# Recurrent stage of a two-block layer: next item's exponential, keys and mask work issued ahead of the current item's output work

## The reference, cut to what matters

```
def step(carry, inp):
    C, n, m = carry
    qc, kc, vc, ic, fc = inp
    b = jnp.cumsum(fc, axis=-1)
    d_log = jnp.where(causal, b[..., :, None] - b[..., None, :] + ic[..., None, :], -jnp.inf)
    m_inter = b + m[..., None]
    m_t = jnp.maximum(m_inter, jnp.max(d_log, axis=-1))
    w_intra = jnp.exp(d_log - m_t[..., None])
    w_inter = jnp.exp(m_inter - m_t)
    s = jnp.einsum('bhld,bhsd->bhls', qc, kc) * w_intra
    num = w_inter[..., None] * jnp.einsum('bhld,bhde->bhle', qc, C) + jnp.einsum('bhls,bhse->bhle', s, vc)
    den = w_inter * jnp.einsum('bhld,bhd->bhl', qc, n) + jnp.sum(s, axis=-1)
    h = num / jnp.maximum(jnp.abs(den), jnp.exp(-m_t))[..., None]
    ...
    C_new = decay[..., None, None] * C + jnp.einsum('bhs,bhsd,bhse->bhde', w_s, kc, vc)
...
hc_f, st_f = mlstm_chunkwise(qc, kc, vc, ifc, lfc, zero)        # context, forward
hl_f, _ = mlstm_chunkwise(ql, kl, vl, ifl, lfl, st_f)           # latent, from that state
...                                                             # and both reversed
out_lat = mlstm_output(hl_f + jnp.flip(hl_b, axis=2), p_lat, g_norm)
```

## Time and profile before

| | us |
|---|---|
| median of three runs | 3012.24 |
| the profiled execution, its own time | 3010.53 |
| its span (first to last instruction) | 3008.7 |
| TensorE busy over the span | 2878.0 (96%) |
| VectorE, ScalarE, GpSimd busy | 2046.6, 1243.9, 144.7 |
| recurrent stage, from its first instruction to the first one behind its barrier | 674.86 to 745.59 |
| of it TensorE's items b(0) to b(15) | 679.65 to 740.8 |
| mean granted TensorE clock over the span | 0.986 of full speed |

### The profile page before, as it was taken

The page is one execution under the profiler, slowest core; times in us unless marked ns, Lnnn a source line. Parts: engine busy times, 40 slices in busy tenths (PEclk is TensorE's granted clock), DMA queues, the critical chain, the costliest instruction groups (busy, mean ns, idle before and its releaser), DMA issues. The chain is left out here.

```text
span 3008.7 us, 38123 instructions
## 1 busy us (share of the span) xinstructions
PE 2878.0 (96%) x14307; PEld 2349.9 (78%) x14307; DVE 2046.6 (68%) x2904; ACT 1243.9 (41%) x2122; POOL 144.7 (5%) x225
## 2 busy tenths in 40 slices
PE   6999999998999999999999999998989999999997
PEld 2587667988778888788787888887878888887786
DVE  3368645837778889997895768774765756775455
ACT  3322535417454555454444332324444224445353
POOL 1100000001010000000001000000001001001000
PEclk9999999998999999999999999999999999999999
DMA  9877045841858778787785646662423544684333
GB/s 359 305 265 246 17 136 158 283 153 35 297 197 268 246 257 255 239 269 256 262 305 173 189 148 175 217 216 64 142 93 131 197 152 150 205 280 125 100 140 131
DMA packets 282967, 589.44 MB, mean 196 GB/s; under 512 B 31090, under 2 KB 64090, under 8 KB 279201
## 3 DMA queue, kind: packets, MB, share of 16 engines
q1 hardware_dynamic: 272384, 546.64, 55.4%
q0 software_dynamic: 10000, 39.72, 3.8%
q10 hardware_dynamic: 400, 0.66, 0.1%
HBM read 572.21 MB, written 14.72 MB: 195 GB/s over the span
## 5 line engine op out<-in xcount | busy, mean ns | idle before, releaser
L3137 DVE TENSOR_TENSOR w_lo<-raw,w_hi 128x1024 fp32r<-128x1024 f32 (+2 forms) x668 | 785.6, 1188 | 384.1 <-ACT w_hi L3108 375.0
L3108 ACT ACTIVATE w_hi<-raw 128x1024 fp32r<-128x1024 f32 (+2 forms) x668 | 677.8, 1031 | 879.9 <-PE bank L3200 630.9
L732 DVE SCALAR_TENSOR_TENSOR acc<-raw,sc_t,acc 128x1024 f32<-128x1024 f32 x480 | 601.8, 1281 | 44.1 <-DMA acc<-in_b_ada 25.1
L3198 PE MATMUL bank<-w_hi,l_hT_hi 128*128 128x512 f32 (+1 forms) x1056 | 390.5, 370 | 10.3 <-DVE w_lo L3137 9.3
L3200 PE MATMUL bank<-w_hi,l_hT_lo 128*128 128x512 f32 (+1 forms) x1056 | 386.9, 366 | 0.0
L3199 PE MATMUL bank<-w_lo,l_hT_hi 128*128 128x512 f32 (+1 forms) x1056 | 386.8, 366 | 0.0
L3198 PE MATMUL bank<-w_hi,f_hT_hi 128*128 128x512 f32 x704 | 278.2, 395 | 1.7 <-DVE mod L780 1.1
L3200 PE MATMUL bank<-w_hi,f_hT_lo 128*128 128x512 f32 x704 | 274.9, 390 | 0.0
L3199 PE MATMUL bank<-w_lo,f_hT_hi 128*128 128x512 f32 x704 | 274.8, 390 | 0.0
L3198 PEld LDWEIGHTS bank<-w_hi,l_hT_hi 128*128 128x128 f32 x1056 | 198.3, 188 | 51.4 <-DVE w_lo L3137 13.1
L3200 PEld LDWEIGHTS bank<-w_hi,l_hT_lo 128*128 128x128 f32 x1056 | 198.2, 188 | 31.5
(11 more groups left out here) (471 smaller groups left out, 4633.2 us busy)
## 6 DMA issues: line engine op xcount, KB each, us to landing
raw<-in_w_in SPq DMA_DIRECT2D x240, 512.0 KB, 4.8
raw<-in_w_mod SPq DMA_DIRECT2D x192, 512.0 KB, 5.5
raw<-in_w_ada SPq DMA_DIRECT2D x192, 512.0 KB, 4.7
raw<-in_w_up SPq DMA_DIRECT2D x176, 512.0 KB, 4.8
raw<-in_w_out SPq DMA_DIRECT2D x96, 512.0 KB, 4.8
raw<-in_w_down SPq DMA_DIRECT2D x88, 512.0 KB, 5.6
raw<-in_w_in SPq DMA_DIRECT2D x32, 288.0 KB, 3.4
raw<-in_w_ukv SPq DMA_DIRECT2D x32, 256.0 KB, 3.4
```

What stands on the lines that cost most here:

```text
L732: e.scalar_tensor_tensor(acc[a][:, :], raw[s % RAW_SLOTS][:, :], scalar, acc[a][:, :], ALU.mult, ALU.add).then_inc(fma_done, 1)
L3108: e.activation(slot(w_hi[u % SPLIT_SLOTS], g.width), slot(raw[s % RAW_SLOTS], g.width), ACT.Copy).then_inc(hi_ready, 1)
L3137: e.tensor_tensor(slot(w_lo[u % SPLIT_SLOTS], g.width), slot(raw[s % RAW_SLOTS], g.width), slot(w_hi[u % SPLIT_SLOTS], g.width).bitcast(F3 ...
L3198: e.matmul(o, xh[:, k, tok], hi[:, kk, :], start=first, stop=False)
```

## The change

Two loops are written in another order; nothing is added or removed, and no semaphore wait is changed. On ScalarE, `c(s-1)` (the scaling of the item before) moves from ahead of the exponential and the keys of item s+1 to behind them. On VectorE, `b(s+1)` (mask times products of the next item) moves from behind the sums of item s-1 to ahead of them.

```
             for s in range(-1, NCH + 2):
                 if s in (3, 5, 7, 9):
                     fill["act"](e, (s - 3) // 2)
-                if 0 <= s - 1 < NCH:
-                    c(s - 1)
                 if s + 1 < NCH:
                     a(s + 1)
                     keys(s + 1)
+                if 0 <= s - 1 < NCH:
+                    c(s - 1)
                 if 0 <= s < NCH:
                     b(s)
@@
                     fill["dve"](e, (s - 4) // 2)
                 if s + 1 < NCH:
                     a(s + 1)
+                    b(s + 1)
                 if 0 <= s - 1:
                     dpart(s - 1)
-                if s + 1 < NCH:
-                    b(s + 1)
                 if s in (5, 9):
                     gained(s // 8)
```

## The result

The changed kernel took 3032.59 us, median of 4 runs (3030.04 to 3033.95), against 3012.15 for the kernel before (4 runs): a ratio of 1.0067, 95% interval 1.0049 to 1.0084. Measured again beside other kernels, with 5 runs against 10, it gave 3030.56 to 3012.02, ratio 1.0063 (1.0051 to 1.0076). It is slower by 20.4 us in the first comparison and by 18.5 in the second. The forecast was 14.4 us, in a range of 7 to 24.

A forecast was written before the change was run, and what follows sets the result against it. TensorE was taken to bound plain rounds before, a chain closing on VectorE after. Fourteen rounds with splits and gains sum to 69.99 us instead of 56.26: 13.8 later, plus 0.6 clock, 14.4 us, giving 3026.6; range 3019.5 to 3036.

The forecast's parts named there:

- A chain that closes on VectorE: Recurrent stage: a plain round runs from VectorE's a through ScalarE to the sums, 4.43 or 4.56 us, mean 4.50.
- so this chain is the one that decides: Exponential, keys, then scaled copies let the sums start 2.86 us after a, later than 2.36 through b and GpSimd.
- The sums: VectorE's sums take 1.57 and 1.70 us by direction, no longer beside GpSimd; 0.48 us less in each of 14.
- Splits and gains on the path: VectorE's four weight splits of 1.14 us and two gains of 1.25 count in full, 7.06 us.
- The clock: TensorE at half speed in the stage: between 0 and 22.7 us more, as gaps hide it or not.
- so I take 0.6, near the lower end: TensorE's half speed adds 0.6 us, a quarter of one late round, as each round has 1.19 us to spare.
- I take the shift to reach the end in full: Behind the recurrent stage nothing changes, so its whole delay shows in the program's time.
- 3024 to 3029.5: Range in us of the program's time for the main forecast alone, without rivals; chance 62%.
- Only the GpSimd chain counts: Rival, 10%: sums start 2.36 us after a, rounds 0.50 us shorter, 7.0 in all, 3019.6 us.
- The sums keep their old length: Rival, 10%: VectorE's sums stay 0.48 us longer in each of 14 rounds, 6.7 us more, 3033.3 us.
- The clock falls in most rounds: Rival, 13%: TensorE at half speed in half of the rounds, 7 us more, 3034 us, far end 3049.

The follow-up runs named there:

- e1: Against the kernel before, only VectorE's b is moved ahead of the sums, ScalarE's order as before: 3016.13 us, ratio 1.0014.
- e3: The changed kernel with ScalarE's scaled copies put between the exponential and the keys: 3016.54 us, ratio 1.0017 to the kernel before.
- e2: Against the kernel before, only ScalarE's scaled copies are moved behind exponential and keys, VectorE's order as before: 3036.17 us, ratio 1.0077.
- v2: The kernel before with the denominator made by four small VectorE instructions of one SBUF tensor each, in place of two with two: 3010.36 us, ratio 0.9996.
- v1: The kernel before with VectorE's two gains moved from rounds 5 and 9 to round 0 and the last: 3006.99 us, ratio 0.9984.
- v4: The kernel before with the gains moved to the first and last rounds and the weight split put behind VectorE's a: 3003.75 us, ratio 0.9971.
- e4: The changed kernel with matmul products of steps a and c repeated to fill TensorE's gaps: 3030.32 us, ratio 1.0061 to the kernel before.

## Why the prediction was right

*A chain that closes on VectorE* (the step "so this chain is the one that decides"): right, and shown from three sides. e1 takes the ScalarE part out and leaves 2.23 us from a to the sums; e3 keeps the exponential in front and gets 2.24 (689.48 - 687.24, in its VectorE rows); e2 keeps the 2.91.

*Its size.* I had 0.64 + 1.56 + 0.66 = 2.86; measured 0.65 + 1.58 + 0.68 = 2.91. The 0.05 in 14 rounds is 0.7 us.

*The sums.* 1.57 and 1.70 us as forecast (686.86 - 685.29, 691.47 - 689.77), L2241 at 0.16 in all 16 items. v2 shows the cause: with one SBUF tensor for each instruction the stall goes although GpSimd's timing is unchanged. The forms of the instructions changed with it, but the form is not it: in before's rounds with a split GpSimd starts later (695.40), and then it is L2242, another form with two SBUF inputs, that takes 0.70 us (from 695.43) instead of 0.16, and L2241 that takes 0.16. That a VectorE instruction with two SBUF inputs and a GpSimd instruction that reads SBUF contend is what the Trainium skill's "SBUF — State Buffer", section "Who interferes with whom", states, and the trace agrees.

In the new order the sums are a part of the closed chain, so their 0.48 us counts in each round. In the old order it doesn't: v2 took the stall away, and plain rounds stayed at 3.3 to 3.4 us.

*Splits and gains on the path*: 1.14 (697.08 - 695.94) and, for a gain, 1.26 as taken.

*The clock* is the term of the stage that was mis-sized. The step "so I take 0.6, near the lower end" took the time to spare in a plain round for cover everywhere. It covered the half-speed stretches at 713 and 724 us, but in round 11, which follows a gain and a split, it didn't. TensorE began b(11) 0.11 us after VectorE's a, as in plain rounds, but at half speed, and stayed there through a(13), which came late: 1.47 us in one profile, 1.26 in the other. And at b(15) nothing is left to spare, since every step there waits for the one ahead: 7.97 instead of 6.43 us in one profile, 6.43 in the other. Together 3.0 us and 1.3 us, where 0.6 was forecast. That the second profile's stage is 2.2 us shorter is mostly this 1.5 at b(15), 0.2 in the late round, and 0.35 in the items 0 and 1, which the change doesn't touch.

The sum from a(2) to b(15) is 72.54 us in the first profile: 69.99 forecast, 0.7 for the chain, 1.5 for the late round, and some tenths for splits (2.96 from a to sums behind them). With b(15)'s 1.5 the stage is 17.8 us longer where the forecast's terms in the stage gave 14.4; in the second profile 15.6.

*The rest of the program*: "I take the shift to reach the end in full" holds in that nothing of it is lost; whether something is added stays open. In the first profile the shift stays between 16.4 and 17.7 us from L992 behind the stage to the start of the last projection. In that projection 3.6 us more appear, where TensorE once waited 2.2 us for VectorE (0.3 before) and the clock fell behind it (0.83 over 10 us). In the second profile the shift moves between 11.4 and 16.2 us on the way, and the last projection adds 3.8. The medians rose by 18.5 and 20.4 us against 15.6 and 17.8 for the stage: 2.6 to 2.9 us are not explained by the stages of these profiles. They can lie behind the stage, or in the one profile of before: its stage has 3.1 to 3.2 us of half speed in it that v1 and v2 don't have (4.94 and 4.95 us against 3.3 to 3.4 for the rounds behind the gains), and executions without it would make the stage's shift larger by that much. No run separates the two.

*What luck there was.* The range held, but the prediction's own "3024 to 3029.5" for the forecast alone did not: 3032.59 and 3030.56 lie above it. 3032.59 is in fact nearest to the rival of the longer sums (3033.3) and that of the clock (3034), and the traces show neither, with L2241 at 0.16 us and plain rounds at full speed. Who had the time alone would have picked a wrong cause. It is the chain with its splits and gains, 14.5 of the 18.5 to 20.4 us, that makes the prediction right; the rest is a clock term two to five times as large as taken, and an open part of 2.6 to 2.9 us.

*The rivals.* "Only the GpSimd chain counts" is what e1 and e3 are, not what the changed kernel is. "The sums keep their old length" is out. "The clock falls in most rounds" is out: plain rounds, with TensorE's pauses of 0.17 and 0.7 to 0.8 us, kept full speed in both profiles (0.99 at 741 to 745 us). What the Trainium skill says in "TensorE: Matmul & The Clock Gate", "HAM oscillation — how this bites in real kernels" of bursts that lose the clock each time is seen in these rounds, in both profiles, only behind waits of 2.1 to 2.5 us, before c(6) and c(10). In one profile it is seen also behind 0.86 us before c(8) and 1.35 before c(14), in the other behind 1.26 before c(4); waits of the same length in the other profile were followed by full speed. So these runs give no length of a wait that decides it.

## What to carry to other kernels

When an instruction is moved ahead on an in-order engine, write down for each engine what is queued behind the new wait, and follow the chain until it meets itself: work with slack (five scaled keys) in front of work without (the copies that the sums need) costs its full length in every round. Two halves of a reordering can each be a loss and still not add up; run them apart. Put work that is needed by nobody soon into the idle time that the timeline shows, the first rounds and the last, and not between rounds of the engine that closes the chain. And before an edit gets the credit for a shorter stage, look up round by round where the time went: in v2 it was the clock in two rounds, and no run shows that the edit brought it.

## What the runs showed of the hardware

A VectorE instruction of 128 x 2 elements took 0.63 us instead of 0.16 when it had two SBUF inputs and a GpSimd multiplication was running; it ended with that one's end. It didn't happen to instructions of 128 x 1 with one SBUF tensor beside the same multiplication (0.20 to 0.22 us, v2). With a split of 128 x 1024 started first on VectorE, GpSimd's instruction took 0.82 to 0.89 us instead of 0.73 (v4).

Repeating matmuls kept TensorE at 2.4 GHz (granted clock 1.00 from 730 to 745 us in e4, against 0.50 from 735 to 740 in the changed kernel) and removed the late round, which had cost 1.47 and 1.26 us. The stage took 85.97 us against 88.54 and 86.35; in the time of the whole no gain is seen. A wait of 1.83 to 1.86 us on TensorE was followed by half speed in the kernel before and by full speed in v2, at the same two places.

The same kernel's executions spread more than three runs showed: the kernel before ranged from 3005.7 to 3016.9 us over 27 runs, and from 3004.7 to 3017.9 over all 60, so a change of 5 us in the time needs the profile of its stage beside the median.
